# Seven products for eight in a few tile pairs of three down projections, of a float32 transformer stack on one Trainium2 core

## The chip, the cores and the metric

One core of a Trainium2 chip runs the whole program. The metric is device microseconds (us) for one execution; lower is better. Engines: PE is TensorE (PEld its weight loads), DVE is VectorE, ACT is ScalarE, POOL is GpSimd, SP is the queue that issues the weight loads from HBM.

## The reference, cut to what matters

Two transformer blocks on 256 tokens of width 2048, in float32. The change lies in the feed-forward of the first:

```python
hn = rms_norm(h, norm_ffn[i])
h = h + jnp.square(jax.nn.relu(hn @ ffn_w1[i])) @ ffn_w2[i]     # 2048 -> 8192 -> 2048
gate = jax.nn.sigmoid(rms_norm(h, norm_ple[i]) @ ple_w_gate[i])
h = h + (p[i] @ ple_w_proj[i]) * gate
```

## The kernel before

**Precision.** A float32 operand is split in two float32r parts, high and low, and a product is three matmuls: high by high, high by low, low by high. With a stationary of 128x128 (tokens) and a moving operand of 128x512 (weights) that is three matmuls of 512 columns for each tile product.

**The weight pipeline.** All weights come as one stream of 756 pieces of 128x1024 (`PW`). For each piece SP loads it to one of four slots of `raw`; ACT writes the high part to `whi` (`split_hi`, L1833), DVE the low part to `wlo` (`split_lo`, L1115). ACT may write piece q when PE has used piece q-4 (`piece_used`); DVE follows ACT; PE waits for `lo_ready`; SP loads piece q+4 when the low part of piece q is written. Every engine has one queue in program order, and all of them walk through the pieces with `rows_body`: at its step s it first splits piece s+3 and then does what is entered for s.

**The feed-forward** is cut in four chunks of 2048 hidden columns, `chunk(c)`: chunk 0, a loop over chunks 1 and 2, then a small projection (`proj`) and chunk 3. A chunk has 64 pieces. Pieces 0 to 31 are the up stage (`ff`): four groups g of 512 hidden columns, 8 pieces each, in `rows_group` (L550 to L552). Behind each group ACT applies the scale and the relu from two PSUM banks to `z` (`ff_relus`, step 8g+7, L2046), DVE turns it by 32x32 transposes (`ff_turn`, steps 8g+8 and 8g+9, L1515), ACT writes the squares' high part to `H` (`ff_squares`, step 8g+10, L2052), and POOL makes the square once more (L2339) and the low part (L2342), tile by tile, four tiles for each g. Pieces 32 to 63 are the down stage (`fd`): 16 tiles of hidden by 2048 columns, two groups of columns interleaved (`mixed_piece`, L829 to L831), then two more (`rows_group`). DVE adds the sums from PSUM to the residual `xN` (`fd_in`, L1537). A piece is 12 matmuls in both stages.

**PSUM.** The up and down stages use banks 0 to 3 in turn; banks 4 to 7 are free in chunks 0 to 2.

Of the kernel before, what the change touches and what calls it, by code (L numbers as in the profile page):

```python
# [179 lines left out]


def turn_of(n):

    return 4 * (n // 3) + TURN_AT[n % 3]


class Steps:
# [5 lines left out]
    def __call__(self, ins):  # L193
        self.n = self.n + 1
        ins.then_inc(self.sem, 1)
        self.eng.wait_ge(self.sem, self.n)


def program(nc, xT, pT, wstream, consts, setup, params, grows, xrows, out):
# [11 lines left out]
    with ExitStack() as ctx:  # L211
# [45 lines left out]
        zr, sq = ring(bflat, 0), ring(bflat, 4 * S, 8)  # L257
        tA, tB, tC = ring(Sm, 0), ring(Sm, 4 * S), ring(Sm, 8 * S)
        ub, c0 = ring(ptf, 0, 4, S + 4), ring(ptf, 4 * (S + 4), 2)
        sq2 = ring(ptf, 0)  # L260
# [84 lines left out]
        var_most, var_half = sem("var_most"), sem("var_half")  # L345
        ff_turned, ff_hi, ff_step, ff_ready = (sem(n) for n in ("ff_turned", "ff_hi", "ff_step", "ff_ready"))
        fd_sq, fd_turned, fd_hi, a2_ready = (sem(n) for n in ("fd_sq", "fd_turned", "fd_hi", "a2_ready"))
        frs_ready = sem("frs_ready")
# [12 lines left out]
        fin_rs, fin_out, out_done = (sem(n) for n in ("fin_rs", "fin_out", "out_done"))  # L361
        dn_half = sem("dn_half")

        NORM_AT = {"kv": 3, "k2": 0, "up0": 6}
# [96 lines left out]
        def _(pe):  # L461
# [73 lines left out]

            def rows_group(p, p0, u, u0, K, src, ready=None, between={}, upper=False):

                for t in range(QT):
                    if not upper:
# [280 lines left out]
            def mixed_piece(p, p0, u0, src, f, h, ready):  # L820
# [11 lines left out]
                last.then_inc(piece_used, 1)  # L832

            def chunk(c):
                ff, fd, o = chunk_at(c)
                first = {0: lambda: turn_wo(3)} if is_chunk(c, 0) else {}
                for f in range(4):
                    rows_group(o * 64 + (PB[ff] + 8 * f), PB[ff] + 8 * f, o * 16 + (UB[ff] + 2 * f), UB[ff] + 2 * f, DT, A,
                               lambda k: (a1_ready, k + 1), first if f == 0 else {})
                for i, (f, h) in enumerate(WO_FIRST):  # L840
                    if h == 0:
                        pe.wait_ge(z_ready, o * 16 + (UB[fd] + 2 * f + QT))
                    mixed_piece(o * 64 + (PB[fd] + i), PB[fd] + i, UB[fd], H, f, h, lambda k: (ff_ready, c * CH + (k + 1)))
                for f in range(2, 4):
                    late = {}
                    if is_chunk(c, FF_CHUNKS - 1):
                        late = {1: lambda: turn_fd(0), 4: lambda: turn_fd(1)} if f == 2 else {2: lambda: turn_fd(2)}
                    rows_group(o * 64 + (PB[fd] + 8 * f), PB[fd] + 8 * f, o * 16 + (UB[fd] + 2 * f), UB[fd] + 2 * f, CH, H, between=late)
# [10 lines left out]
            for f in range(4):  # L859
                rows_group(PB["proj"] + f, PB["proj"] + f, UB["proj"] + 2 * f, UB["proj"] + 2 * f, 2, pA, upper=(f >= 2))  # L860
            chunk(FF_CHUNKS - 1)
# [247 lines left out]
        def _(dve):  # L1109
            V = nc.vector  # L1110
            dve.sem_inc(z_ready, UB["kv"] + 4)

            def split_lo(i, s):
                dve.wait_ge(hi_ready, i + 1)
                V.tensor_tensor(wlo[:, s, :], raw[:, s, :], whi[:, s, :].bitcast(F32), ALU.subtract).then_inc(lo_ready, 1)  # L1115

# [97 lines left out]

            def rows_body(p, p0, per, groups, evac, between={}, short=0):

                for q in range(LEAD, per * groups + AHEAD):
                    if AHEAD <= q < per * groups + AHEAD - short:
                        split_lo(p + q, (p0 + q) % SLOTS)
                    if q - LEAD in between:  # L1220
# [308 lines left out]
            def chunk(c):  # L1529
# [14 lines left out]
                steps_of.update({32 + WO_FIRST.index((f, 7)): lambda f=f: fd_in(f) for f in range(2)})  # L1544
                steps_of.update({32 + 8 * f + 7: lambda f=f: fd_in(f) for f in range(2, 4)})
                if is_chunk(c, FF_CHUNKS - 1):
                    steps_of.update({51: lambda: fd_lo(0), 54: lambda: fd_lo(1), 60: lambda: fd_lo(2)})
                rows_body(p, PB[ff], 64, 1, lambda f: None, steps_of)

# [10 lines left out]
            def proj_in(f):  # L1560

                if f:
                    dve.wait_ge(z_ready, 4 + UB["proj"] + 2 * f)
                V.tensor_copy(yN[:, 0, f * WIDE:f * WIDE + WIDE], psum[(UB["proj"] + 2 * f) % 4 + f // 2 * 4][:, :]).then_inc(z_ready, 1)
            rows_body(PB["proj"], PB["proj"], 1, 4, proj_in)
# [257 lines left out]
        def _(act):  # L1823
# [5 lines left out]

            def split_hi(i, s, lap):  # L1830
                act.wait_ge(raw_landed[s], lap)
                act.wait_ge(piece_used, i + 1)
                C.copy(whi[:, s, :], raw[:, s, :]).then_inc(hi_ready, 1)  # L1833

            def split(p, p0, i, per, it):

                q = p0 + i
                split_hi(p + i, q % SLOTS, (it * (per // SLOTS) + (q // SLOTS + 1)) * 16)

# [18 lines left out]

            def rows_body(p, p0, it, pieces, between={}, short=0):

                for q in range(LEAD, pieces + AHEAD):
                    if AHEAD <= q < pieces + AHEAD - short:
                        split(p, p0, q, pieces, it)
                    if q - LEAD in between:
# [122 lines left out]
            for i in range(ATT_PIECES + 2):  # L1987
# [31 lines left out]
                if i == 44:  # L2019
                    act.dma_start(tC[:, 0:2, :], pT).then_inc(in_p, 16)  # L2020
                    act.dma_start(gfrow, grows[0].partition_broadcast(P)).then_inc(in_gf, 16)

# [31 lines left out]
            def chunk(c):  # L2054
# [7 lines left out]
                if is_chunk(c, FF_CHUNKS - 1):  # L2062
                    steps_of.update({48: lambda: fd_squares(0), 49: lambda: fd_squares(1), 50: lambda: fd_hi_of(0), 53: lambda: fd_hi_of(1),
                                     56: lambda: fd_squares(2), 59: lambda: fd_hi_of(2)})
                rows_body(PB[ff] + o * 64, PB[ff], o, 64, steps_of)

# [218 lines left out]
        def _(pool):  # L2285
# [226 lines left out]
```

## Time and profile before

| | |
|---|---|
| median of 3 runs | 2207.76 us (2206.84 to 2209.46) |
| the profiled execution's own time | 2206.0 us |
| its span, first to last instruction | 2204.1 us |
| PE busy | 2190.7 us, 99% |
| DVE, ACT, POOL busy | 1518.2, 1092.7, 550.8 us |
| moved by DMA | 414.52 MB, mean 188 GB/s |
| granted TensorE clock | 0.999 |

A busy share says how long an engine had an instruction running. A matmul's duration reaches past the start of the next one, so the rate is read from starts, not from durations. The views named below are the page of the profile, groups of instructions by line, waits by engine, and timelines of one engine.

### The profile page before, as it was taken

How to read it: one execution, taken by the hardware profiler on the slowest of the kernel's cores; microseconds unless marked ns; L12 is line 12 of the kernel's file. 1: busy time of each engine (PE TensorE's matmuls, PEld its weight loads, DVE VectorE, ACT ScalarE, POOL GpSimd, SP SyncE). 2: the span in 40 equal slices, each digit the busy share in tenths (PEclk: the TensorE clock that was granted, in tenths of full speed). 3: DMA queues.
4: the chain of work that ended last, by engine and by line, in shares of the span. 5: the costliest groups of instructions: out<-in, count | busy, mean ns of one | idle time of the engine just before them, and what ended most of it. 6: DMA issues, size and time to landing. Idle time of an engine off the chain costs nothing.

```text
span 2204.1 us, 32431 instructions
## 1 busy us (share of the span) xinstructions
PE 2190.7 (99%) x11111; PEld 1852.5 (84%) x11111; DVE 1518.2 (69%) x2114; ACT 1092.7 (50%) x1622; POOL 550.8 (25%) x467
## 2 busy tenths in 40 slices
PE   9999999999999999999999999999999999999998
PEld 7888988888888788888888887888888888888887
DVE  6877765685586487578566667577774688756875
ACT  6445555544444344444555455465553455434553
POOL 3202220241051043025000033005540244303431
PEclk9999999999999999999999999999999999999999
DMA  7665335556565556556555654545655555555554
GB/s 258 228 228 167 110 130 205 185 178 212 178 204 198 182 181 210 182 183 210 189 182 187 222 167 136 197 155 188 200 190 191 191 190 189 190 194 191 187 208 149
DMA packets 118093, 414.52 MB, mean 188 GB/s; under 512 B 12896, under 2 KB 18048, under 8 KB 117472
## 3 DMA queue, kind: packets, MB, share of 16 engines
q1 hardware_dynamic: 111600, 401.37, 54.0%
q10 hardware_dynamic: 6384, 11.70, 1.7%
q8 instruction: 69, 1.13, 0.2%
q14 instruction: 40, 0.33, 0.0%
HBM read 409.29 MB, written 2.15 MB: 187 GB/s over the span
## 4 chain that ended last, share of the span: by engine, by line
PE 96%; DVE 1%; DMA 1%; POOL 1%; ACT 1%; issue 0%; DVEq 0%; ACTq 0%; SPq 0%; POOLq 0%
PE bank L493 22%; PE bank L501 12%; PE bank L550 10%; PE bank L552 10%; PE bank L551 10%; PE bank L1075 4%; PE bank L1076 4%; PE bank L1074 4%; PE bank L829 3%; PE bank L830 3%; PE bank L831 3%; PE bank L626 1%; PE bank L1009 1%; PE bank L663 1%; PE bank L803 1%; PE bank L805 1%
## 5 line engine op out<-in xcount | busy, mean ns | idle before, releaser
L1115 DVE TENSOR_TENSOR wboth<-raw,wboth 128x1024 fp32r<-128x1024 f32 x756 | 986.0, 1312 | 540.5 <-ACT wboth L1833 538.9
L1833 ACT CAST wboth<-raw 128x1024 fp32r<-128x1024 f32 x756 | 789.4, 1049 | 721.7 <-PE bank L552 231.3
L493 PE MATMUL bank<-A,wboth 128*128 128x512 f32 x1904 | 459.8, 392 | 0.3 <-DVE wboth L1115 0.3
L493 PEld LDWEIGHTS bank<-A,wboth 128*128 128x128 f32 x1904 | 349.2, 188 | 67.8 <-issue 1.0
L501 PEld LDWEIGHTS bank<-A,wboth 128*128 128x128 f32 x1904 | 245.1, 191 | 9.7
L550 PE MATMUL bank<-wboth,A 128*128 128x512 f32 x640 | 250.2, 391 | 2.1 <-issue 1.7
L501 PE MATMUL bank<-A,wboth 128*128 128x256 f32 x1904 | 250.8, 284 | 0.0
L552 PE MATMUL bank<-wboth,A 128*128 128x512 f32 x640 | 249.5, 390 | 0.0
L551 PE MATMUL bank<-wboth,A 128*128 128x512 f32 x640 | 249.3, 390 | 0.0
L2339 POOL TENSOR_TENSOR Sm<-Sm 128x256 f32<-128x256 f32 x64 | 100.9, 1577 | 540.5 <-DVE Sm L1515 540.5
L2296 POOL TENSOR_TENSOR PT<-z,rs 128x256 f32<-128x256 f32 x88 | 73.4, 835 | 465.4 <-DVE z L1146 464.8
L550 PEld LDWEIGHTS bank<-wboth,A 128*128 128x128 f32 x640 | 120.2, 188 | 27.4 <-DVE wboth L1115 1.7
L551 PEld LDWEIGHTS bank<-wboth,A 128*128 128x128 f32 x640 | 120.3, 188 | 25.9 <-issue 1.6
L552 PEld LDWEIGHTS bank<-wboth,A 128*128 128x128 f32 x640 | 120.2, 188 | 25.1
L1076 PE MATMUL bank<-wboth,H 128*128 128x512 f32 x352 | 137.1, 389 | 0.0
L1074 PE MATMUL bank<-wboth,H 128*128 128x512 f32 x352 | 137.1, 389 | 0.0
L1075 PE MATMUL bank<-wboth,H 128*128 128x512 f32 x352 | 137.1, 389 | 0.0
L550 PE MATMUL bank<-wboth,H 128*128 128x512 f32 x320 | 125.2, 391 | 0.0
L552 PE MATMUL bank<-wboth,H 128*128 128x512 f32 x320 | 124.8, 390 | 0.0
L551 PE MATMUL bank<-wboth,H 128*128 128x512 f32 x320 | 124.6, 389 | 0.0
L1515 DVE STREAM_TRANSPOSE Sm<-z 32x256 f32<-32x256 f32 x256 | 111.5, 436 | 4.2
L829 PE MATMUL bank<-wboth,H 128*128 128x512 f32 x256 | 99.9, 390 | 0.0
(299 smaller groups left out, 2990.9 us busy)
## 6 DMA issues: line engine op xcount, KB each, us to landing
raw<-wstream SPq DMA_DIRECT2D x756, 512.0 KB, 3.3
bias<-bias_rows ACTq DMA_DIRECT2D x6, 512.0 KB, 5.3
x<-xrows ACTq DMA_DIRECT2D x1, 2048.0 KB, 9.1
bias<-grows ACTq DMA_DIRECT2D x2, 1024.0 KB, 5.7
out<-x SPq DMA_DIRECT2D x8, 256.0 KB, 2.1
x<-xT SPq DMA_DIRECT2D x7, 256.0 KB, 5.2
pA<-bias_rows ACTq DMA_DIRECT2D x2, 512.0 KB, 10.1
Sm<-grows ACTq DMA_DIRECT2D x1, 1024.0 KB, 6.1
```

Of the source, the lines that this page charges most:

```text
L493: last = nc.tensor.matmul(bank(j)[:, :], whi[:, s, cols(i)], moving(j, k), start=(k == 0), stop=(k == K - 1))
L501: last = nc.tensor.matmul(bank(j)[:, 0:S], wlo[:, s, cols(i)], moving(j, k)[:, 0, :], start=False, stop=False)
L550: nc.tensor.matmul(bank[:, :], src[:, k, 0, tok], whi[:, s, w], start=(k == 0), stop=False)
L551: nc.tensor.matmul(bank[:, :], src[:, k, 0, tok], wlo[:, s, w], start=False, stop=False)
L552: last = nc.tensor.matmul(bank[:, :], src[:, k, 1, tok], whi[:, s, w], start=False, stop=(k == K - 1))
L829: nc.tensor.matmul(bank[:, :], src[:, k, 0, tok], whi[:, p0 % SLOTS, w], start=(k == 0), stop=False)
L1074: nc.tensor.matmul(bank[:, :], H[:, k, 0, tok], whi[:, s, w], start=(k == 0), stop=False)
L1075: nc.tensor.matmul(bank[:, :], H[:, k, 0, tok], wlo[:, s, w], start=False, stop=False)
L1076: return nc.tensor.matmul(bank[:, :], H[:, k, 1, tok], whi[:, s, w], start=False, stop=(k == n - 1))
L1115: V.tensor_tensor(wlo[:, s, :], raw[:, s, :], whi[:, s, :].bitcast(F32), ALU.subtract).then_inc(lo_ready, 1)
L1515: last = V.transpose(cols[:, :, :, 32 * i:32 * i + 32], rows[:, :, :, 32 * j:32 * j + 32])
L1833: C.copy(whi[:, s, :], raw[:, s, :]).then_inc(hi_ready, 1)
```

## The change

Chunks 0 to 2 take another down stage, `down_pair`. The weights come by pairs of column groups: a piece is one hidden tile by 1024 columns, 16 pieces for each of two column pairs (`cp`). For two of the eight pairs of hidden tiles (`FAST`: pairs 3 and 5) the eight tile products (two token tiles, two hidden tiles, two column groups) become seven products of sums of blocks. In each chunk four groups of pieces are of that kind; they begin at pieces 38, 42, 54 and 58 (`X_AT`). The sums:

- of hidden tiles (`mix`): three small sums on POOL behind its four tiles of g = 1 and g = 2, a high part of 128x512 on ACT (`mix_high`, steps 22 and 30), a low part on POOL.
- of weights (`t_first`, `t_rest`): two sums of 128x512 on DVE at step x-4, two on POOL; the high parts on ACT in two halves at step x-2 (`t_highs`), the low parts on DVE before it splits piece x+2 (`t_lows`). Before DVE splits piece x+1 it waits for POOL's two.
- of results: the seventh products stand in four extra PSUM banks, `side_bank`. DVE adds them at steps 44 and 60 (`sides_in`), POOL makes three more adds (`corners`), DVE adds the main banks (`mains_in`). Main and side banks swap between the two column pairs, so all eight are used.

Of pieces 38, 42, 54 and 58 only the first half is split. The projection swaps its two halves of PSUM, and the load of a 1 MB row of gains (`gfrow`) moves from the attention to just ahead of the projection. Chunk 3 stays as it was.

```diff
+FAST = ((3, 5), (3, 5))
+MIXED = sorted({m for ms in FAST for m in ms})
+GROUPS = [(cp, n, m) for cp, ms in enumerate(FAST) for n, m in enumerate(ms)]
+X_AT = {32 + 16 * cp + 2 * m: g for g, (cp, n, m) in enumerate(GROUPS)}
...
+                def group(i, g):
+
+                    _, n, m = GROUPS[g]
+                    lone, final = n == 0, n == len(FAST[cp]) - 1
...
+                    product(side_bank(cp, ONE), *hidden(i, early), *weights(i, 0), lone, final).then_inc(piece_used, 1)
+                    arrive(i + 1)
+                    product(main_bank(cp, 0), *hidden(i + 1, early), *weights(i + 1, 0))
+                    pe.wait_ge(*mix_ready.at(c * len(MIXED) + (MIXED.index(m) + 1)))
+                    product(main_bank(cp, 2), *mix_of(m, 3), *weights(i + 1, 1)).then_inc(piece_used, 1)
+                    pe.wait_ge(*t_lo.at(2 * group_of(c, g) + 1))
+                    product(side_bank(cp, FIVE), *mix_of(m, 1), *sums(0), lone, final)
+                    product(side_bank(cp, SEVEN), *mix_of(m, 0), *sums(1), lone, final)
+                    pe.wait_ge(*t_lo.at(2 * group_of(c, g) + 2))
+                    product(side_bank(cp, SIX), *mix_of(m, 2), *sums(2), lone, final)
+                    product(main_bank(cp, 1), *hidden(i + 1, late), *sums(3)).then_inc(t_used.sem, 1)
...
+                if cp:
+                    for i in (14, 15):
+                        arrive(i)
+                        last = plain(i, 0)
+                    last.then_inc(first_half.sem, 1)
+                    for i in (14, 15):
+                        plain(i, 1).then_inc(piece_used, 1)
```

DVE:

```diff
+                steps_of.update({x - 4: lambda x=x, g=g: t_first(c, x, g) for x, g in X_AT.items()})
+                ahead = {x + 1: lambda g=g: dve.wait_ge(*t_more.at(2 * group_of(c, g) + 2)) for x, g in X_AT.items()}
+                ahead.update({x + 2: lambda g=g: t_lows(c, g) for x, g in X_AT.items()})
+                steps_of.update({44: lambda: sides_in(c, 0), 49: lambda: mains_in(c, 0, range(4)), 60: lambda: sides_in(c, 1),
+                                 62: lambda: mains_in(c, 1, range(2)), 63: lambda: mains_in(c, 1, range(2, 4))})
+                rows_body(p, PB[ff], 64, 1, lambda f: None, steps_of, 0, ahead, X_AT)
```

ACT:

```diff
+                steps_of.update({8 * (m // 2) + 14: lambda n=n, m=m: mix_high(c, n, m) for n, m in enumerate(MIXED)})
+                steps_of.update({x - 2: lambda g=g: t_highs(c, g) for x, g in X_AT.items()})
+                steps_of.update({44: lambda: copy_side(c, 0), 60: lambda: copy_side(c, 1)})
...
+            def mix_high(c, n, m):
+
+                act.wait_ge(*mix_sum.at(c * 3 * len(MIXED) + (3 * n + 3)))
+                if not is_chunk(c, 0):
+                    act.wait_ge(*t_used.at(group_of(c, 0)))
+                C.copy(mixed[0][:, m // 2, :, :], mixsum[:, m // 2, :, :]).then_inc(mix_hi.sem, 1)
+
+            def t_highs(c, g):
+
+                act.wait_ge(*t_sum.at(2 * group_of(c, g) + 2))
+                if g or not is_chunk(c, 0):
+                    act.wait_ge(*t_used.at(group_of(c, g)))
+                C.copy(Tcopy[0][:, 0:2, :], Tsum[:, 0:2, :]).then_inc(t_hi.sem, 1)
+                act.wait_ge(*t_more.at(2 * group_of(c, g) + 2))
+                C.copy(Tcopy[0][:, 2:4, :], Tsum[:, 2:4, :]).then_inc(t_hi.sem, 1)
```

POOL, in `chunk(c)`:

```diff
                         G.tensor_tensor(part(H, 4 * g + j, 1), tB[:, j, :], part(H, 4 * g + j, 0).bitcast(F32),
                                         ALU.subtract).then_inc(ff_ready, 1)
+                    if 2 * g + 1 in MIXED and not is_last(c):
+                        mix(c, MIXED.index(2 * g + 1), g)
+                if not is_last(c):
+                    for cp in range(2):
+                        for x, g in X_AT.items():
+                            if GROUPS[g][0] == cp and x > 34:
+                                t_rest(c, x, g)
+                        corners(c, cp)
...
+            def mix(c, n, g):
...
+                G.tensor_tensor(dst[:, 0:2, :], ends_of, a[:, late].unsqueeze(1).to_broadcast([P, 2, P]), ALU.subtract).then_inc(mix_sum.sem, 1)
+                pool.wait_ge(*mix_sum.at(s0 + 1))
+                G.tensor_tensor(dst[:, 2, :], dst[:, 1, :], a[:, early], ALU.add).then_inc(mix_sum.sem, 1)
+                pool.wait_ge(*mix_sum.at(s0 + 2))
+                G.tensor_tensor(dst[:, 3, :], b[:, early], dst[:, 2, :], ALU.subtract).then_inc(mix_sum.sem, 1)
+                pool.wait_ge(*mix_sum.at(s0 + 3))
+                pool.wait_ge(*mix_hi.at(c * len(MIXED) + (n + 1)))
+                G.tensor_tensor(mixed[1][:, g, :, :], dst, mixed[0][:, g, :, :].bitcast(F32), ALU.subtract).then_inc(mix_ready.sem, 1)
```

## Rows read from the trace of the kernel before

**Rows 1.** The page: busy time of engines, granted clock in 40 slices.

```profile
PE 2190.7 (99%) x11111; PEld 1852.5 (84%) x11111; DVE 1518.2 (69%) x2114; ACT 1092.7 (50%) x1622; POOL 550.8 (25%) x467
...
PEclk9999999999999999999999999999999999999999
```

**Rows 2.** PE's waits from 390 to 1100 us: total, times, longest.

```profile
PE bank L550 <- issue: 1.7, 2, 1.4
```

**Rows 3.** PE's timeline: start us, duration us, engine, instruction.

```profile
473.05 0.40 PE L550 MATMUL bank<-wboth,A 128*128 128x512 f32 x1
...
481.23 0.39 PE L829 MATMUL bank<-wboth,H 128*128 128x512 f32 x1
...
481.91 0.39 PE L829 MATMUL bank<-wboth,H 128*128 128x512 f32 x1
```

**Rows 4.** ACT's timeline in chunk 0, groups g = 1 and 2.

```profile
450.98 2.93 ACT L1833 CAST wboth<-raw 128x1024 fp32r<-128x1024 f32 x3
454.43 1.05 ACT L1833 CAST wboth<-raw 128x1024 fp32r<-128x1024 f32 x1 [0.51 <-DMA raw<-wstream]
456.98 1.05 ACT L1833 CAST wboth<-raw 128x1024 fp32r<-128x1024 f32 x1 [1.51 <-PE bank L552]
459.65 1.27 ACT L2046 ACTIVATE z<-bank,nrm 128x512 f32<-128x512 f32 x2 [1.62 <-PE bank L552]
460.80 1.05 ACT L1833 CAST wboth<-raw 128x1024 fp32r<-128x1024 f32 x1
```

**Rows 5.** POOL's timeline: end of g = 1, then g = 2 and 3.

```profile
458.68 1.59 POOL L2339 TENSOR_TENSOR Sm<-Sm 128x256 f32<-128x256 f32 x1
460.35 0.73 POOL L2342 TENSOR_TENSOR H<-Sm,H 128x256 fp32r<-128x256 f32 x1
...
482.15 0.74 POOL L2342 TENSOR_TENSOR H<-Sm,H 128x256 fp32r<-128x256 f32 x1
493.37 1.65 POOL L2339 TENSOR_TENSOR Sm<-Sm 128x256 f32<-128x256 f32 x1 [10.48 <-DVE Sm L1515]
...
503.94 0.74 POOL L2342 TENSOR_TENSOR H<-Sm,H 128x256 fp32r<-128x256 f32 x1
```

**Rows 6.** POOL's timeline in chunk 1, a square with DVE idle.

```profile
654.85 0.61 POOL L2339 TENSOR_TENSOR Sm<-Sm 128x256 f32<-128x256 f32 x1
```

**Rows 7.** DVE's timeline in chunk 0, g = 2 and 3.

```profile
452.05 7.75 DVE L1115 TENSOR_TENSOR wboth<-raw,wboth 128x1024 fp32r<-128x1024 f32 x5 [1.09 <-ACT wboth L1833]
461.88 1.23 DVE L1115 TENSOR_TENSOR wboth<-raw,wboth 128x1024 fp32r<-128x1024 f32 x1 [2.08 <-ACT wboth L1833]
463.02 3.59 DVE L1515 STREAM_TRANSPOSE Sm<-z 32x256 f32<-32x256 f32 x8
...
471.54 1.22 DVE L1115 TENSOR_TENSOR wboth<-raw,wboth 128x1024 fp32r<-128x1024 f32 x1
...
489.68 3.61 DVE L1515 STREAM_TRANSPOSE Sm<-z 32x256 f32<-32x256 f32 x8
```

**Rows 8.** DVE's timeline in chunk 0, splits of pieces 37 to 42.

```profile
493.32 1.23 DVE L1115 TENSOR_TENSOR wboth<-raw,wboth 128x1024 fp32r<-128x1024 f32 x1
495.64 7.75 DVE L1115 TENSOR_TENSOR wboth<-raw,wboth 128x1024 fp32r<-128x1024 f32 x5 [1.09 <-ACT wboth L1833]
```

**Rows 9.** Groups by line and shape: busy us, mean ns, idle before.

```profile
L1537 DVE TENSOR_TENSOR x<-x,bank 128x512 f32<-128x512 f32 x32 | 20.6, 684 | 6.1 <-PE bank L831 3.1 <-PE bank L552 3.1
...
L2326 POOL TENSOR_TENSOR Sm<-Sm,small 128x512 f32<-128x512 f32 x16 | 20.0, 1267 | 24.2 <-DVE small L1292 24.1
...
L1580 DVE TENSOR_TENSOR y<-x,Sm 128x512 f32<-128x512 f32 x8 | 5.5, 691 | 0.3
...
L1949 ACT CAST wboth<-raw 128x512 fp32r<-128x512 f32 x1 | 0.6, 604 | 0.0
```

More of the change, by code:

```diff
@@ L534, in spread_rs, with rows_group @@
                 nc.tensor.matmul(psum[4][:, 0:S], ones[:, :], acc[:, :], start=True, stop=True).then_inc(sum_ready, 1)
-            def rows_group(p, p0, u, u0, K, src, ready=None, between={}, upper=False):
+            def rows_group(p, p0, u, u0, K, src, ready=None, between={}, upper=False, free=False):
                 for t in range(QT):
-                    if not upper:
+                    if not free:
                         pe.wait_ge(z_ready, u + t + 1)
@@ L832, in mixed_piece, with product, down_pair, weights @@
                 last.then_inc(piece_used, 1)
+            def product(bank, a_hi, a_lo, w_hi, w_lo, start=False, stop=False):
+                nc.tensor.matmul(bank[:, :], a_hi, w_hi, start=start, stop=False)
+                nc.tensor.matmul(bank[:, :], a_hi, w_lo, start=False, stop=False)
+                return nc.tensor.matmul(bank[:, :], a_lo, w_hi, start=False, stop=stop)
+            def down_pair(c, cp):
+                _, fd, o = chunk_at(c)
+                p, z0 = o * 64 + (PB[fd] + 16 * cp), o * 16 + (4 + UB[fd])
+                early, late = slice(0, P), slice(P, 2 * P)
+                def weights(i, f):
+                    s, w = (PB[fd] + 16 * cp + i) % SLOTS, slice(f * WIDE, f * WIDE + WIDE)
+                    return whi[:, s, w], wlo[:, s, w]
+                def hidden(i, tok):
+                    return H[:, i, 0, tok], H[:, i, 1, tok]
+                def mix_of(m, i):
+                    return mixed[0][:, m // 2, i, :], mixed[1][:, m // 2, i, :]
+                def sums(i):
+                    return Tcopy[0][:, i, :], Tcopy[1][:, i, :]
+                def arrive(i):
+                    pe.wait_ge(lo_ready, p + (i + 1))
+                    if cp == 0:
+                        pe.wait_ge(ff_ready, c * CH + (i + 1))
+                def plain(i, f):
+                    for t in range(QT):
+                        last = product(main_bank(cp, 2 * f + t), *hidden(i, slice(t * P, t * P + P)), *weights(i, f), i == 0, i == 15)
+                    return last
+                def group(i, g):
+                    _, n, m = GROUPS[g]
+                    lone, final = n == 0, n == len(FAST[cp]) - 1
+                    if lone and cp == 0:
+                        pe.wait_ge(z_ready, z0)
+                    if lone and cp:
+                        pe.wait_ge(*banks_taken.at(c * 8 + 4))
+                    product(side_bank(cp, ONE), *hidden(i, early), *weights(i, 0), lone, final).then_inc(piece_used, 1)
[10 more added lines that the diff above has]
+                if cp:
+                    pe.wait_ge(z_ready, z0 + 4)
+                elif not is_chunk(c, 0):
+                    pe.wait_ge(*banks_taken.at(c * 8))
+                for i in range(16 - 2 * cp):
+                    g = X_AT.get(32 + 16 * cp + i)
+                    if X_AT.get(32 + 16 * cp + i - 1) is not None:
+                        continue
+                    arrive(i)
+                    if g is not None:
+                        group(i, g)
+                    else:
+                        plain(i, 0)
+                        plain(i, 1).then_inc(piece_used, 1)
+                if cp:
+                    for i in (14, 15):
+                        arrive(i)
+                        last = plain(i, 0)
+                    last.then_inc(first_half.sem, 1)
+                    for i in (14, 15):
+                        plain(i, 1).then_inc(piece_used, 1)
@@ L1213, in take_rs, with rows_body @@
                     dve.wait_ge(rs_ready, then)
[L1215 removed]
+            def rows_body(p, p0, per, groups, evac, between={}, short=0, ahead={}, halves=()):
                 for q in range(LEAD, per * groups + AHEAD):
+                    if q in ahead:
+                        ahead[q]()
                     if AHEAD <= q < per * groups + AHEAD - short:
[L1219 removed]
+                        split_lo(p + q, (p0 + q) % SLOTS, WIDE if q in halves else PW)
                     if q - LEAD in between:
@@ new lines, in t_lows, with sides_in @@
+            def t_lows(c, g):
+                for h in range(2):
+                    two = slice(2 * h, 2 * h + 2)
+                    dve.wait_ge(*t_hi.at(2 * group_of(c, g) + (h + 1)))
+                    V.tensor_tensor(Tcopy[1][:, two, :], Tsum[:, two, :], Tcopy[0][:, two, :].bitcast(F32), ALU.subtract).then_inc(t_lo.sem, 1)
+            def sides_in(c, cp):
+                _, fd, o = chunk_at(c)
+                done = banks_taken.sem if cp else z_ready
+                dve.wait_ge(*t_used.at(group_of(c, len(FAST[0]) + (len(FAST[1]) if cp else 0))))
+                if cp or not is_chunk(c, 0):
+                    dve.wait_ge(*corners_added.at(c * 6 + 3 * cp))
+                one, five, six, seven = (side_bank(cp, j)[:, :] for j in range(4))
+                V.tensor_tensor(quarter(cp, 1, 0), quarter(cp, 1, 0), seven, ALU.add).then_inc(done, 1)
+                V.tensor_tensor(quarter(cp, 1, 1), quarter(cp, 1, 1), seven, ALU.subtract).then_inc(done, 1)
+                dve.wait_ge(*side_copied.at(c * 2 + (cp + 1)))
+                V.tensor_tensor(quarter(cp, 0, 0), quarter(cp, 0, 0), one, ALU.add).then_inc(done, 1)
+                V.tensor_tensor(corner, six, cross, ALU.subtract).then_inc(side_step.sem, 1)
+                dve.wait_ge(*side_step.at(c * 2 + (cp + 1)))
+                V.tensor_tensor(cross, corner, five, ALU.subtract).then_inc(done, 1)
@@ L1857, in body, with rows_body @@
                                     step(j)
-            def rows_body(p, p0, it, pieces, between={}, short=0):
+            def rows_body(p, p0, it, pieces, between={}, short=0, halves=()):
                 for q in range(LEAD, pieces + AHEAD):
                     if AHEAD <= q < pieces + AHEAD - short:
-                        split(p, p0, q, pieces, it)
+                        split(p, p0, q, pieces, it, WIDE if q in halves else PW)
                     if q - LEAD in between:
@@ L2335, in chunk @@
                 for g in range(4):
+                    if g == 3 and 34 in X_AT and not is_last(c):
+                        t_rest(c, 34, X_AT[34])
                     pool.wait_ge(ff_turned, c * 16 + (4 * g + 4))
```

132 lines of the change are left out of this document (112 added, 20 removed).

## The prediction

> **What bounds the kernel.** I read the page first. PE is busy for 2190.7 of 2204.1 us and the granted clock stands at 9 in all forty slices, which is the 2.4 GHz level [rows 1]. Then PE's waits in the four chunks: 1.7 us at the turn of the loop, and nothing above 0.3 us besides [rows 2]. So fewer matmuls are worth their full time, as long as no other engine falls behind.
>
> The timelines tell how near that is. The start of one triple and of the next in the down stage are 481.23 and 481.91: 0.227 us for a matmul, 2.72 us for a piece of twelve. The down stage of chunk 0 begins at 481.23, so piece 29 begins at 481.23 - 3 x 2.72 = 473.07, and a row shows it at 473.05 [rows 3]. DVE ends the low part of piece 29 at 471.54 + 1.22 = 472.76 [rows 7]: 0.3 us ahead. In the same way piece 37 begins at 481.23 + 5 x 2.72 = 494.83 and its low part is done at 493.32 + 1.23 = 494.55 [rows 8]: 0.3 us again. The reader is to see that after each group's relu and transposes DVE has no lead left, though it is busy for only 69% of the span [rows 1]. The chain is: relu (ACT), low part of the next piece and eight transposes, a low part, eight transposes, a low part (DVE). Whatever delays the relu by more than 0.3 us delays PE.
>
> **What it removes.** Each group of two pieces has 21 matmuls in place of 24. Four groups in three chunks: 12 x 3 x 0.227 = 8.2 us off PE. Shapes and strides of the matmuls are those of before, so I give each the 0.227 us.
>
> **First wait: the sums of hidden tiles, at g = 1 and g = 2.** ACT is to make the high part at step 22, that is behind the split of piece 25 at 454.43 and ahead of the split of piece 26 (456.98) and of the relu of g = 2 (459.65) [rows 4]. It waits there for three sums that POOL makes only behind its four tiles of g = 1, and these end at 460.35 + 0.73 = 461.08 [rows 5]. Queued behind the waiting ACT are the split of piece 26, the relu, and piece 27.
>
> Step by step: DVE lacks piece 26's high part and idles from 452.05 + 4 x 1.55 = 458.25 [rows 7], so POOL's last square takes 0.61 us [rows 6] instead of 1.59 and its last low part ends at 460.1. Of the sums one has 256 columns, 0.74 us as L2342, and two have 128. For these no row stands; from 0.74 at 256 and 1.27 at 512 [rows 9] I estimate 0.47 each. With some 0.08 us between instructions the sums end at 462.0. High part 0.60 [rows 9], piece 26 1.05, relu 1.27 with piece 27 beginning 1.15 after it, piece 27 1.05 [rows 4]: DVE can start piece 27 at 465.95, where it started at 461.88 [rows 7]. That is 4.1 us late, of which 0.3 are covered: 3.8 us of PE. Piece 26 itself costs nothing more, since its low part (464.9) comes when PE reaches it (464.9).
>
> At g = 2 the same happens: POOL ends its tiles at 482.15 + 0.74 = 482.9 [rows 5], 21.8 us behind g = 1 as all else, and the high part is at step 30. DVE and POOL have both moved by the first delay, and nothing is covered now: 4.1 us. Bounds for each of the two: 3.2 us if the small sums cost next to nothing, 5.5 us if POOL shares its time with DVE, since a square takes 1.59 us beside DVE's splits and 0.61 alone [rows 5, 6].
>
> The Trainium skill (GPSIMD Engine Reference, Specifications) says that POOL's way into SBUF is shared with VectorE and contended by DVE instructions that have two SBUF inputs. The splits are such, and the trace agrees (1.59 against 0.61 us). By that rule a waiting DVE makes POOL quick, which gives the lower of my two prices, about 4 us; if POOL had the same speed whatever DVE does, each wait would be 5.5 us and the whole some 9 us longer.
>
> **Second wait: the sums of weights at piece 38.** DVE may not split piece 39 before POOL has made its two sums, and these stand in POOL's queue behind all four tiles of g = 3. Call T the end of the last transposes (489.68 + 3.61 = 493.29 before [rows 7]). POOL began those tiles at 493.37 and ended them at 503.94 + 0.74 = 504.68, or T + 11.4 [rows 5]; PE reaches the second matmul triple of piece 38 at 494.83 + 2.72 + 0.68 = 498.23, T + 4.9.
>
> With the change: DVE's low part of 37 ends at T + 1.3, the two sums (0.69 each, as L1580 [rows 9]) at 2.65, half of piece 38 at 3.35, and then it waits. POOL's first tile and the start of the second run beside DVE: 1.65 + 1.6 us. The rest runs alone: 0.61 + 0.74 with 0.05 between, 1.4 us a tile, so the fourth ends at T + 7.6. The two sums have 512 columns, 1.27 us each [rows 9] and one waits for the other: T + 10.4. Low part of 39: T + 11.65. PE started piece 37 at T + 1.3, piece 38 at 4.0, and stands after three matmuls at 4.7: **7.0 us of wait**. The 18 other matmuls end at T + 15.8; DVE has by then made both low parts of the sums (12.9, 14.1) and piece 40 (15.3), so nothing is added. ACT, which waits for the same POOL, gives the high parts at 11.5 and 12.6. Bounds: 5 us (POOL's sums at half price), 9 us (its tiles at the pace beside DVE for longer).
>
> **The other three groups.** For piece 42 the same queue has POOL free: DVE's sums, half a split, POOL's 2.8 us, then piece 43. I count 0.4 us of wait, since DVE had just caught up. For 54 and 58 DVE has its full lead of about three pieces (8 us), of which two sums, POOL and two low parts of 1.23 us take about 6: no wait; with POOL slowed, up to 1 us.
>
> **Results.** Five adds of 0.68 us (L1537 [rows 9]) at step 44 and at step 60 are 3.4 us, beside four plain pieces of PE (10.9 us). At the end of a chunk the first two main banks must be free for the next up stage: PE gives them 12 matmuls (2.72 us) ahead, DVE needs 2 x 0.68 and about 0.4 of signal: 1 us to spare. If that cover were gone it would cost its excess, three times. `corners` is POOL's, DVE waits for it at step 49 with about two pieces of lead. The 1 MB row of gains is some 5 us of DMA between pieces that land 5 us ahead of need: nothing. The projection's swap of banks waits for adds that are past by then: nothing. The order of weights changes no byte. Half splits of 12 pieces save ACT and DVE time that is off the path.
>
> **Sum.** Per chunk 3.8 + 4.1 + 7.0 + 0.4 = 15.3 us; three chunks 45.9; less 8.2: **+37.7 us**. Against the profiled execution: 2206.0 + 37.7 = 2243.7 us, and the median stands 1.8 above it: 2245.5 us.
>
> **Rivals.**
>
> - *Only the wait at piece 38 bites.* If ACT's wait for the small sums were covered (POOL being done earlier than its rows say), 3 x 7.4 - 8.2 = +14: 2222 us. Against it: POOL's end at 461.08 is 1.4 us behind the relu that it now holds, and DVE has 0.3 us. Chance 0.10.
> - *The clock falls in the waits.* Before, PE never stands over 1.7 us in these chunks and the granted clock never leaves 2.4 GHz, so no row shows what 7 us of rest do. At the 1.2 GHz level a matmul costs 0.227 us more; if the 18 behind each long wait ran so, 3 x 18 x 0.227 = +12 us: 2258 us. Part of that would hide behind DVE's own work in the same stretch (3.6 us of the 4.1). The Trainium skill (TensorE: Matmul & The Clock Gate, Part 1) says that a TensorE without work is throttled to half rate until it has been busy again for a while; by it this rival would hold, and its price is the one above. Chance 0.12.
> - *None of the waits bites: faster.* 2207.8 - 8.2 = 2199.6 us. One thing decides it: POOL, whose spans are rough. It is so if POOL has finished g = 3 and its two sums by T + 3.4, 7 us ahead of my reckoning; between, the change breaks even where a chunk waits 2.7 us in all. Four tiles at the fastest rows, 1.4 us each, already take 5.6 us. Chance 0.06.
> - *No change*, the waits near 2.7 us a chunk: 0.02.
>
> **Numbers.** The forecast has 0.70. With bounds: 3 x (3.2 + 3.2 + 5.0 + 0) - 8.2 = +26, 2234 us, and 3 x (5.5 + 5.5 + 9 + 2) - 8.2 = +58, 2266 us. The range takes in the first rival below and the clock's above: 2221 to 2262 us. What this kernel's measurement can tell from no change is about 0.2%, 4.4 us. Faster 0.06, within 0.2% 0.02, slower 0.92.
>
> **What would show it.** In the profile after: PE's waits should list, three times each, about 7 us at the triple behind piece 38's first (releaser DVE's split L1115), and two smaller groups of waits, 4 us in all each, at pieces 28 and 29 and at 36 and 37. ACT's high part of the hidden sums should wait for POOL, and relu rows should come about 4 us later against the up stage's end of g. POOL's squares of g = 3 should shrink from 1.59 to 0.61 us. PE should have 36 matmuls fewer and its pitch of 0.227 us kept. The prediction is wrong if PE does not wait at piece 39 although POOL's second weight sum ends late, or if POOL's rows of the trace are not where its work ended.

## The result and the profile after

| | before | after |
|---|---|---|
| median | 2208.05 us (4 runs) | 2246.86 us (4 runs, 2246.29 to 2247.87) |
| profiled execution, own time / span | 2206.0 / 2204.1 us | 2247.87 / 2246.0 us |
| mean granted clock | 0.999 | 0.991 |

The changed kernel takes 1.018 times as long, 95% interval [1.0168, 1.0192]; the medians are 38.8 us apart. Forecast were 2245.5 us. The profiled execution is the longest of the four, 1.0 us above their median.

The page of the changed kernel first, against [rows 1]:

```profile
PE 2199.5 (98%) x11075; PEld 1851.4 (82%) x11075; DVE 1572.6 (70%) x2192; ACT 1115.0 (50%) x1658; POOL 620.7 (28%) x533
...
PEclk9999999999999998999999999999999999999999
```

PE has 36 matmuls fewer and is busy for 8.8 us longer: the busy time of a matmul grows when its clock is low, and the clock's row has an 8 now. PE's waits from 385 to 1110 us, against [rows 2] (total, times, longest):

```profile
PE bank L893 <- DVE wboth L1260: 24.2, 10, 6.2
PE bank L607 <- DVE wboth L1260: 9.0, 9, 1.9
PE bank L607 <- ACT y L2316: 0.8, 1, 0.8
PE bank L607 <- issue: 0.6, 1, 0.6
```

L893 is the down stage, L607 the up stage, L1260 the split of the weights that was L1115: 33 us of waiting where there was next to none. More than that was lost, 41.9 + 8.2 = 50.1 us: a listed wait is counted from the modelled end of the matmul before it (0.39 us behind its start, where the next one would start after 0.227), the first start behind a wait comes some 0.1 us slower, and time at a low clock is no wait. The starts of the stages in PE's timeline place it all:

| us from first matmul to the next stage's | before | after | more |
|---|---|---|---|
| up stages of chunks 0, 1, 2 | 88.0, 87.2, 89.0 | 91.9, 91.0, 92.9 | 3.9, 3.8, 3.9 |
| down stages of chunks 0, 1, 2 | 87.0, 87.6, 87.2 | 97.3, 97.8, 96.4 | 10.2, 10.2, 9.3 |
| projection | 11.4 | 11.9 | 0.5 |

The sum is 41.7 of the 41.9 us between the two spans. The start of piece 37 divides the down stages: up to it, where the delay of g = 2 ends, PE is later by 3.6, 3.7 and 2.1 us, and from there to the end by 6.6, 6.5 and 7.2 us although 2.7 us of matmuls are gone, so that 9.4, 9.2 and 9.9 us are lost there. Chunk 2 has other parts: the 3.9 us of its up stage are 3.7 up to piece 29 and 1.8 of low clock behind it, less 1.6 us (1.4 as the list counts) that PE had waited at the loop's turn before [rows 2] and now does not; coming late by the clock, PE waits less in the down stage.

The projection's 0.5 us is one of ACT's copies that PE waits for (0.8 us here, 0.3 before); ahead of it a split by DVE beside POOL's `corners` of chunk 2 took 1.71 us and not 1.23. No run tried what made the copy late.

**The wait on ACT, chunk 0, g = 1 to 2.** ACT's timeline, which stands against [rows 4], then POOL's against [rows 5], then DVE's against [rows 7]:

```profile
454.79 1.06 ACT L2038 CAST wboth<-raw 128x1024 fp32r<-128x1024 f32 x1 [0.53 <-DMA raw<-wstream]
462.24 0.62 ACT L2288 CAST vT<-kT 128x512 fp32r<-128x512 f32 x1 [6.40 <-POOL kT L2599]
462.77 1.04 ACT L2038 CAST wboth<-raw 128x1024 fp32r<-128x1024 f32 x1
463.72 1.26 ACT L2250 ACTIVATE z<-bank,nrm 128x512 f32<-128x512 f32 x2
```

```profile
459.00 0.61 POOL L2575 TENSOR_TENSOR Sm<-Sm 128x256 f32<-128x256 f32 x1
459.70 0.74 POOL L2578 TENSOR_TENSOR H<-Sm,H 128x256 fp32r<-128x256 f32 x1
460.39 0.74 POOL L2595 TENSOR_TENSOR kT<-Sm 128x256 f32<-128x256 f32 x1
461.21 0.46 POOL L2597 TENSOR_TENSOR kT<-kT,Sm 128x128 f32<-128x128 f32 x1
461.75 0.46 POOL L2599 TENSOR_TENSOR kT<-Sm,kT 128x128 f32<-128x128 f32 x1
```

```profile
465.94 1.23 DVE L1260 TENSOR_TENSOR wboth<-raw,wboth 128x1024 fp32r<-128x1024 f32 x1 [0.63 <-ACT wboth L2038]
467.09 3.60 DVE L1662 STREAM_TRANSPOSE Sm<-z 32x256 f32<-32x256 f32 x8
...
475.61 1.22 DVE L1260 TENSOR_TENSOR wboth<-raw,wboth 128x1024 fp32r<-128x1024 f32 x1
```

The reader is to see three engines handing on one delay: ACT idles for 6.40 us until POOL's third small sum, its relu comes at 463.72 instead of 459.65, DVE splits piece 27 at 465.94 instead of 461.88 and piece 29 at 475.61 instead of 471.54. Each is 4.1 us late.

**The wait on POOL, chunk 0, piece 38.** Here T, the end of the last transposes, is 497.50 + 3.61 = 501.11. POOL's timeline, DVE's, PE's:

```profile
501.19 1.65 POOL L2575 TENSOR_TENSOR Sm<-Sm 128x256 f32<-128x256 f32 x1 [11.42 <-DVE Sm L1662]
...
508.17 0.72 POOL L2578 TENSOR_TENSOR H<-Sm,H 128x256 fp32r<-128x256 f32 x1
508.85 1.26 POOL L2608 TENSOR_TENSOR PT<-PT,raw 128x512 f32<-128x512 f32 x1
510.19 1.26 POOL L2610 TENSOR_TENSOR PT<-PT,raw 128x512 f32<-128x512 f32 x1
```

```profile
497.50 3.61 DVE L1662 STREAM_TRANSPOSE Sm<-z 32x256 f32<-32x256 f32 x8
...
503.31 1.23 DVE L1714 TENSOR_TENSOR PT<-raw 128x512 f32<-128x512 f32 x1
...
511.48 1.23 DVE L1260 TENSOR_TENSOR wboth<-raw,wboth 128x1024 fp32r<-128x1024 f32 x1 [5.92 <-POOL PT L2610]
```

```profile
502.42 0.50 PE L893 MATMUL bank<-wboth,H 128*128 128x512 f32 x1 [1.88 <-DVE wboth L1260]
...
504.77 0.63 PE L895 MATMUL bank<-wboth,H 128*128 128x512 f32 x1
505.20 0.63 PE L893 MATMUL bank<-wboth,H 128*128 128x512 f32 x1
...
512.76 0.79 PE L893 MATMUL bank<-wboth,H 128*128 128x512 f32 x1 [5.03 <-DVE wboth L1260]
...
514.21 0.63 PE L893 MATMUL bank<-wboth,vT 128*128 128x512 f32 x1
514.63 0.63 PE L894 MATMUL bank<-wboth,vT 128*128 128x512 f32 x1
...
519.24 0.39 PE L893 MATMUL bank<-wboth,H 128*128 128x512 f32 x1
```

POOL's second sum ends at 511.45, T + 10.3; DVE idles 5.92 us for it and splits piece 39 at T + 10.4. PE's starts are 0.43 us apart at 504.77, and again at 514.21: the clock is at its lower level. Piece 40 begins at 519.24, T + 18.1. The windows of the same stretch (us, then busy time of each engine, granted clock, DMA share, GB/s):

```profile
504.00:508.00 4.00, 3.73 (x10) 2.55 (x8) 1.56 (x2) 1.04 (x1) 3.84 (x5) 0.58 0.61 200
508.00:512.00 4.00, 0.00 (x0) 0.00 (x0) 0.52 (x1) 0.52 (x1) 3.29 (x4) 0.85 0.10 39
512.00:516.00 4.00, 3.24 (x8) 2.56 (x9) 4.00 (x4) 2.94 (x4) 0.00 (x0) 0.50 0.41 131
```

Granted are 0.58 and 0.50 of 2.4 GHz, so 1.2 GHz for most of the first and all of the last. It fell first behind waits of 0.88 and 1.88 us, the second of which ended 4.9 us after the first, and was low again behind the 5.03. Of the 18 matmuls behind the long wait 11 start at the low pace in chunk 0, 9 in chunk 1 and 14 in chunk 2; the clock is back before the group ends.

### The profile page after: what moved, and what is told of

Its sections match the earlier page's. It is cut to its first block, busy times and chain, and to the rows that moved or that the text cites. A ratio compares the mean times of both kernels' runs of the same rounds, so it can differ in the third digit from the quotient of the medians.

```text
span 2246.0 us, 32721 instructions
## 1 busy us (share of the span) xinstructions
PE 2199.5 (98%) x11075; PEld 1851.4 (82%) x11075; DVE 1572.6 (70%) x2192; ACT 1115.0 (50%) x1658; POOL 620.7 (28%) x533
## 4 chain that ended last, share of the span: by engine, by line
PE 71%; issue 20%; POOL 6%; DVE 1%; ACT 1%; DMA 0%; POOLq 0%; DVEq 0%; ACTq 0%
PE bank L550 22%; PE bank L558 12%; PE bank L1220 4%; PE bank L1221 4%; PE bank L1219 4%; PE bank L607 3%; PE bank L609 3%; PE bank L608 3%; POOL Sm L2575 2%; POOL H L2578 1%; PE bank L893 1%; PE bank L894 1%; PE bank L895 1%; PE bank L663 1%; PE bank L664 1%
## 5 line engine op out<-in xcount | busy, mean ns | idle before, releaser
L1260 DVE TENSOR_TENSOR wboth<-raw,wboth 128x1024 fp32r<-128x1024 f32 x756 | 979.0, 1303 | 530.5 <-ACT wboth L2038 487.2
L607 PE MATMUL bank<-wboth,A 128*128 128x512 f32 x640 | 251.6, 393 | 10.4 <-DVE wboth L1260 9.0
L2530 POOL TENSOR_TENSOR PT<-z,rs 128x256 f32<-128x256 f32 x88 | 73.5, 836 | 465.5 <-DVE z L1291 464.9
L2575 POOL TENSOR_TENSOR Sm<-Sm 128x256 f32<-128x256 f32 x64 | 88.5, 1382 | 328.3 <-DVE Sm L1662 328.3
L607 PEld LDWEIGHTS bank<-wboth,A 128*128 128x128 f32 x640 | 120.5, 188 | 40.5 <-DVE wboth L1260 9.2
L893 PE MATMUL bank<-wboth,H 128*128 128x512 f32 x312 | 124.8, 400 | 24.3 <-DVE wboth L1260 24.2
L1220 PE MATMUL bank<-wboth,H 128*128 128x512 f32 x352 | 136.9, 389 | 0.0
L1219 PE MATMUL bank<-wboth,H 128*128 128x512 f32 x352 | 136.9, 389 | 0.0
L1221 PE MATMUL bank<-wboth,H 128*128 128x512 f32 x352 | 136.9, 389 | 0.0
L894 PE MATMUL bank<-wboth,H 128*128 128x512 f32 x312 | 123.6, 396 | 0.0
L895 PE MATMUL bank<-wboth,H 128*128 128x512 f32 x312 | 123.3, 395 | 0.0
L1291 DVE TENSOR_REDUCE z<-bank 128x256 f32<-128x512 f32 x108 | 74.2, 689 | 27.5 <-PE bank L550 27.3
```

The costliest lines, as they stand in the source:

```text
L893: nc.tensor.matmul(bank[:, :], a_hi, w_hi, start=start, stop=False)
L894: nc.tensor.matmul(bank[:, :], a_hi, w_lo, start=False, stop=False)
L1219: nc.tensor.matmul(bank[:, :], H[:, k, 0, tok], whi[:, s, w], start=(k == 0), stop=False)
L1220: nc.tensor.matmul(bank[:, :], H[:, k, 0, tok], wlo[:, s, w], start=False, stop=False)
L1221: return nc.tensor.matmul(bank[:, :], H[:, k, 1, tok], whi[:, s, w], start=False, stop=(k == n - 1))
L1260: V.tensor_tensor(wlo[:, s, 0:w], raw[:, s, 0:w], whi[:, s, 0:w].bitcast(F32), ALU.subtract).then_inc(lo_ready, 1)
```

## The experiments

Every time is a median. Every ratio is against the kernel before as it ran beside the experiment, with its 95% interval. That kernel's own median was 2208.05 us beside the change, 2205.94 beside e1 to e4, 2207.94 beside e5 to e7 and 2206.51 beside e8 and e9. So a difference between two kernels of different groups is uncertain by some 2 us; where it matters, the difference of the excesses over the kernel before stands with it.

**e1: ACT makes the high part of the hidden sums three steps later.**

```diff
-                steps_of.update({8 * (m // 2) + 14: lambda n=n, m=m: mix_high(c, n, m) for n, m in enumerate(MIXED)})
+                steps_of.update({8 * (m // 2) + 17: lambda n=n, m=m: mix_high(c, n, m) for n, m in enumerate(MIXED)})
```

> One edit: ACT makes the high part of the hidden sums three steps later (25 and 33), behind the relu and the split of piece 28 or 36. Theory (ACT, waiting for POOL, holds the relu, and DVE has no lead): the waits at pieces 28/29 and 36/37, 3.7 us each in the trace of the change, go, 3 x 7.4 = 22 us, and the low clock behind the wait at piece 37 with them; the wait at piece 39 stays near 5 to 7 us. 2221 to 2226 us. Rival (the sums' load on POOL and ACT is what costs, wherever it stands): the time stays within 3 us of 2247.

Measured: 2224.17 us, ratio 1.0084 [1.0068, 1.0099]. ACT's timeline:

```profile
459.37 1.27 ACT L2250 ACTIVATE z<-bank,nrm 128x512 f32<-128x512 f32 x2 [1.61 <-PE bank L609]
...
463.73 0.62 ACT L2288 CAST vT<-kT 128x512 fp32r<-128x512 f32 x1 [0.53 <-POOL kT L2599]
```

The same sums now cost ACT 0.53 us of idling, and the up stages are about as long as before (88.1, 87.5, 87.7 us against 88.0, 87.2, 89.0, of which the last held 1.6 us more at the loop's turn). 22.7 us are back, as expected (20.6 by the excesses, 18.2 us in place of 38.8), and the rival falls: it is the order, not the work. The wait at piece 39 is longer in the record, 6.2 us, since the products ahead of it now run at full clock.

**e2: POOL makes the weight sums of pieces 38 and 42 earlier**, between its tiles.

```diff
-                    if g == 3 and 34 in X_AT and not is_last(c):
-                        t_rest(c, 34, X_AT[34])
+                    if g == 3 and 38 in X_AT and not is_last(c):
+                        t_rest(c, 38, X_AT[38])
...
                     for j in range(4):
+                        if g == 3 and j == 2 and not is_last(c):
+                            t_rest(c, 42, X_AT[42])
...
-                            if GROUPS[g][0] == cp and x > 34:
+                            if GROUPS[g][0] == cp and x > 42:
```

> One edit, on POOL alone: its two weight sums for piece 38 stand ahead of the four tiles of g = 3, and those for piece 42 between the second tile and the third. Theory (DVE waits at piece 39 for POOL's queue): the sums end at T + 5.7 instead of T + 11.4 or 10.4, T being the end of the last transposes; the wait at piece 39 falls from 5.0 us at its recorded length to about 2.3, the 15 to 20 matmuls at half clock around it are mostly gone; waits at 28/29 and 36/37 stay. 2223 to 2231 us. Rival (POOL's sums are slow wherever they stand, because DVE shares its way): the wait moves to pieces 42 to 45 and the time stays above 2238.

Measured: 2234.81 us, ratio 1.0132 [1.0117, 1.0148]. A miss by half: 12 us back (9.9 by the excesses) instead of 16 to 24, above my window and below the rival's. DVE's timeline shows why:

```profile
506.09 1.62 DVE L1260 TENSOR_TENSOR wboth<-raw,wboth 128x1024 fp32r<-128x1024 f32 x1 [2.54 <-POOL PT L2612]
507.63 3.31 DVE L1721 TENSOR_TENSOR Tboth<-PT,Tboth 128x1024 fp32r<-128x1024 f32 x2
510.86 2.89 DVE L1260 TENSOR_TENSOR wboth<-raw,wboth 128x1024 fp32r<-128x1024 f32 x2
```

The wait for POOL is 2.54 us. But POOL's tiles now run beside DVE's group work: a split takes 1.62 us and the two low parts 3.31, where in the changed kernel they took 1.23 and 2.35. A second wait of 0.7 us follows at piece 43 in chunks 0 and 1. PE's wait at piece 39 was to be 2.3 us; it is so in chunk 2 alone (2.28). In chunks 0 and 1 it is 0.66, because the clock still fell ahead of it, behind the waits at pieces 36 and 37, and PE came late.

**e3: both edits.**

> Both edits. If the two waits are separate mechanisms in series the gains add: 2208 - 8.2 + 3 x 2.3 = 2207 us, between 2203 and 2211; if they are one, the time is that of the better of the two, 2221 or more.

Measured: 2213.81 us, ratio 1.0033 [1.0021, 1.0045]. The gains add, 22.7 and 12.1 against 33.1 us for both (20.6 and 9.9 against 30.9 by the excesses), so the two waits are separate; the time is 7 us above the forecast and 3 us outside its window. Its up stages are as before; its down stages are longer by 2.4, 2.8 and 2.8 us where I had 2.3 - 2.7 = -0.4. Waits of 2.2 to 2.3 us at piece 39 and 0.7 at 43 in two chunks explain 0.7 of that; the rest are late starts of up to 0.3 us each inside the groups, some 1.9 us a down stage, and in chunk 2 six matmuls at the lower clock.

**e4: both edits, and no group at piece 38**; **e9** is the same kernel once more, beside e8.

```diff
-FAST = ((3, 5), (3, 5))
+FAST = ((5,), (3, 5))
```

> Both edits, and the pair at piece 38 is left to the plain eight products: three groups a chunk instead of four, 27 matmuls fewer than before instead of 36. Theory: 2208 - 6.1 and no wait left over 0.5 us: 2202 to 2204 us, faster than both kernels. Rival (a group costs more at its own place than the 0.68 us it saves): no faster than the kernel before.

> The three groups with both orders mended once more, on the same chip as the one above, to compare the two: 2201 us, 0.2% below the kernel before; the other is faster only if its fourth group costs less than 0.68 us a chunk.

Measured: 2201.21 us, ratio 0.9977 [0.9968, 0.9986]; again 2201.33 us, ratio 0.9973 [0.9963, 0.9983]. PE's waits from 385 to 1010 us hold no split any more:

```profile
PE bank L607 <- ACT y L2316: 0.8, 1, 0.8
PE bank L607 <- issue: 0.6, 1, 0.6
```

This version is faster than both kernels, than the one before by 0.2%. The seven products give most of what they save once no split is waited for: 27 matmuls are 6.1 us, 4.7 and 5.2 us are measured. Half a microsecond of the rest is PE's wait for ACT's copy in the projection, which stands here too.

**e5: PE works through the long wait.**

```diff
                     product(side_bank(cp, ONE), *hidden(i, early), *weights(i, 0), lone, final).then_inc(piece_used, 1)
+                    if g == 0:
+                        for _ in range(22):
+                            nc.tensor.matmul(side_bank(cp, SIX)[:, :], A[:, 0, 0, 0:P], A[:, 0, :, :], start=True, stop=True)
                     arrive(i + 1)
```

> The changed kernel, and behind the first three matmuls of piece 38 PE runs 22 matmuls on operands at hand into the bank of the sixth product, whose own first product starts that bank anew later; they fill 5.0 us of the wait and compute nothing that is used. Theory (the engine's rest lets the granted clock fall to 1.2 GHz, and the products behind run at half the pace): the clock stays at 2.4 GHz through piece 38, the end of group 38 comes at T + 15.8 instead of T + 18.1, and the time falls by 3 x 2.3 = 7 us, to 2240 us (2237 to 2243). Rival (the low clock hides behind DVE's own steps, as the prediction had it for most): 2245 to 2249 us.

Measured: 2239.56 us, ratio 1.0148 [1.0132, 1.0163], 7.3 us less than the changed kernel (7.2 by the excesses) with 66 matmuls more. Here T is 500.46. The windows of the wait and of the products behind it, and PE's first matmul of piece 40:

```profile
508.00:512.00 4.00, 2.92 (x13) 2.07 (x12) 1.07 (x1) 1.07 (x2) 2.81 (x3) 1.00 0.00 0
512.00:516.00 4.00, 3.79 (x17) 3.13 (x18) 4.00 (x5) 2.94 (x4) 0.00 (x0) 1.00 0.34 133
```

```profile
516.44 0.39 PE L893 MATMUL bank<-wboth,H 128*128 128x512 f32 x1
```

The clock stays at 1.00, and DVE splits piece 39 at 510.93, T + 10.5, where the changed kernel has T + 10.4. DVE's wait is the same, only the clock of PE behind it differs. Piece 40 begins at T + 16.0, 16.1 and 16.1 us in the three chunks, in the changed kernel at T + 18.1, 18.0 and 18.9: 2.1, 1.8 and 2.8 us, 6.7 of the 7.3. The low clock does not hide.

**e6: the list of pairs alone.** The edit of e4 without the two orders.

> Only the list of pairs: the pair at piece 38 takes the plain eight products, orders on ACT and POOL stay as in the change. Theory: the waits at 28/29 and 36/37 stay (7.4 us a chunk), the wait at 39 is gone, and the group at 42, whose POOL sums stand behind the tiles of g = 3, waits little (under 1 us): 2206 + 3 x (7.4 + 1.2 of low clock - 2.0) + 1 = 2227 us, 2222 to 2231. Rival (piece 38 is no special place; the wait moves to piece 43): 2240 us or more.

Measured: 2224.57 us, ratio 1.0073 [1.0057, 1.0088]. The waits at pieces 28, 29, 36 and 37 stand (8.7 us in the up stages, 7.6 in the down stages, all but 0.6 us at these four), and there is none at 39 nor at 43, though POOL's sums for 42 still stand behind its tiles. The clock falls here without any long wait, once in each chunk. A window of chunk 0, behind the waits of 0.87 and 1.88 us at pieces 36 and 37; then, in chunk 1, the wait at piece 37 with none at 36 ahead of it, and the window behind it:

```profile
504.00:508.00 4.00, 3.88 (x10) 3.10 (x11) 2.92 (x4) 3.00 (x4) 3.84 (x4) 0.57 0.50 147
```

```profile
685.56 0.49 PE L893 MATMUL bank<-wboth,H 128*128 128x512 f32 x1 [1.89 <-DVE wboth L1260]
```

```profile
688.00:692.00 4.00, 4.00 (x19) 3.33 (x18) 4.00 (x3) 2.01 (x3) 3.84 (x4) 1.00 0.71 201
```

**e7: four groups, the fourth at piece 50; both orders mended.**

```diff
-FAST = ((3, 5), (3, 5))
+FAST = ((5,), (1, 3, 5))
...
-                steps_of.update({44: lambda: sides_in(c, 0), 49: lambda: mains_in(c, 0, range(4)), 60: lambda: sides_in(c, 1),
+                steps_of.update({44: lambda: sides_in(c, 0), 48: lambda: mains_in(c, 0, range(4)), 60: lambda: sides_in(c, 1),
```

> Four groups a chunk again, with the fourth at piece 50 (pair 1 in the second column pair) instead of 38, both orders mended, and the main banks of the first column pair taken in a step earlier (48). Theory (a group costs nothing where DVE has its lead and POOL is free): 36 matmuls fewer, 2206 - 8.2 + 1 to 2 of loose ends = 2199 us, 2197 to 2201. Rival (with three groups in sixteen pieces DVE's lead is used up, or PE waits at piece 50 for the main banks): 2203 us or more.

Measured: 2216.65 us, ratio 1.0041 [1.0027, 1.0055]: a miss. PE waits 3.4 to 3.5 us at piece 50 in every chunk, for the adds of the main banks, L1753. DVE's timeline:

```profile
528.38 0.68 DVE L1260 TENSOR_TENSOR wboth<-raw,wboth 128x512 fp32r<-128x512 f32 x1
531.62 1.23 DVE L1260 TENSOR_TENSOR wboth<-raw,wboth 128x1024 fp32r<-128x1024 f32 x1 [2.56 <-POOL PT L2612]
532.76 2.47 DVE L1753 TENSOR_TENSOR x<-x,bank 128x512 f32<-128x512 f32 x4
```

The rival had named this wait; its cause I had not counted: DVE waits for POOL's weight sums of piece 50 at its step for piece 51, and the adds stand right behind.

**e8: the same with the main banks taken one step earlier,** ahead of that wait (47 instead of 48).

> As the kernel with a group at piece 50, but DVE takes the main banks of the first column pair at step 47 instead of 48, that is before it waits for POOL's weight sums of piece 50. Theory (the 3.4 us wait at piece 50 is the order in DVE's queue: mains behind the wait for POOL): the wait falls to 0 to 1 us a chunk, the low clock behind it goes, 2216.7 - 3 x (3 to 3.5) - 3 to 6 of clock: 2200 to 2204 us. Rival (POOL's corner adds end too late for any order): 2212 us or more.

Measured: 2202.01 us, ratio 0.9980 [0.9971, 0.9989]:

```profile
526.75 0.68 DVE L1260 TENSOR_TENSOR wboth<-raw,wboth 128x512 fp32r<-128x512 f32 x1
527.36 2.47 DVE L1753 TENSOR_TENSOR x<-x,bank 128x512 f32<-128x512 f32 x4
530.01 1.23 DVE L1260 TENSOR_TENSOR wboth<-raw,wboth 128x1024 fp32r<-128x1024 f32 x1 [0.18 <-POOL PT L2612]
```

The adds fill the time in which DVE waited for POOL (0.18 us instead of 2.56 are left). 14.6 us come back from one step's place (13.2 by the excesses). Of waits for splits 1.0 us is left in three places. Beside e9 (2201.33 us) there is no difference that the measurement can tell: the fourth group's 2.0 us are spent. Its three down stages together are 0.4 us longer than e9's, where 2.0 less was due; 1.0 of that is those waits, and the rest stays without a place.

## Why the prediction was right, point by point

- **That nothing else bounds the kernel, and 8.2 us off PE.** Right: 36 matmuls fewer, the same 0.227 us between starts at full clock; e4 bears it out, with 4.7 and 5.2 of 6.1 us.
- **The first wait, 3.8 us at g = 1.** Measured 3.9, 3.8, 3.9 us in the three up stages, the last of other parts, as said above. The steps of the sum held to 0.4 us: POOL's sums end at 462.2 (forecast 462.0), the low part of piece 26 at 465.3 (464.9, so that it did cost PE 0.3 us), piece 27's split starts at 465.94 (465.95); 128 columns take 0.46 us (0.47). The cause is shown by e1.
- **The same at g = 2, 4.1 us.** Measured 3.6 and 3.7 us in chunks 0 and 1, and 2.1 in chunk 2, where PE came late by the clock. The last transposes end at 501.11 and not 493.29: DVE is 7.8 us late in all, 4.1 since g = 1 and 3.8 more since g = 2. The 4.1 hold 0.3 us by which this execution ran later already (POOL begins the tiles of g = 1 at 450.12, before at 449.78), so each wait held DVE for 3.8 us where the sum had 4.1. The waits (0.88 and 1.88 us in chunk 0) are like those at g = 1 (0.92 and 1.92).
- **The second wait.** DVE splits piece 39 at T + 10.4, as forecast. One step under it was wrong without effect: DVE's two sums, beside POOL's tiles, took 1.10 and 1.23 us and not 0.69 each, which its wait for POOL swallowed. The recorded waits are 5.0, 5.2 and 6.2 us and not 7.0; in chunks 0 and 1 the matmuls ahead ran at half pace and came late themselves. At full clock it is 6.2 us in e1 too: PE stands from T + 5.3 there and not from 4.7. Cause shown by e2 and by e6.
- **The group's end, T + 15.8.** The step that failed: it is T + 18.1, 18.0 and 18.9. The forecast let the products behind the wait run at full clock and gave the low clock to a rival of chance 0.12, saying that part of it would hide. The clock did fall in each chunk, which is that rival's mechanism. The rival charged 4.1 us a group, 18 matmuls at the low pace; 11, 9 and 14 ran so, which is 1.8 to 2.8 us, and e5 shows that none of it hid. So the forecast's term, nothing for the clock, was 7 us short and the rival's 12 us were 5 too many. With the clock kept up (e5) the group ends at T + 16.0 to 16.1: the rest of that sum was right.
- **0.4 us at piece 42, 0 to 1 us at 54 and 58.** No wait there; 1.2 us of the forecast were not spent.
- **Results and projection at nothing.** Right but for 0.5 us in the projection.
- **The sum.** 37.7 us forecast, 41.9 between the spans, 38.8 between the medians. The clock's 7 us stand against smaller losses at g = 2 (2.9 us in all), no wait at 42 (1.2) and a shorter wait at the loop's turn. That the median came out within 1.4 us is in part luck: errors of opposite sign, and a median that rose by 3 us less than the span of the profiled executions did. The stated range, up to 2262 us, also left out the sum of the upper bounds, 2266.
- **POOL beside a waiting DVE.** Of POOL's four squares of g = 3 the first took 1.65 us and the second 1.06 beside DVE's work, the last two 0.61 with DVE waiting; I had 1.65 and 1.6 for the first and the start of the second. The Trainium skill (GPSIMD Engine Reference, Specifications) has the SBUF interfaces shared between the two and contended by DVE instructions with two SBUF inputs: the trace agrees.
- **The clock behind a rest.** Behind the long wait the granted clock was 0.50. The Trainium skill (TensorE: Matmul & The Clock Gate, Part 1) has a TensorE without work throttled: the trace agrees, and e5 shows the price here.

What stays open is when the short waits bring the clock down. That they can is shown by e6: with the waits at pieces 28 and 29 and at 36 and 37 and no long one, the clock fell once a chunk, each time behind such a pair. In e1, without them, it fell once a chunk behind the long wait alone, and in e4 it stayed up. But in the changed kernel and in e6 alike only three of five such pairs were followed by a fall; the one in the up stage of chunk 0 was not, in either. Two lone waits of 1.9 us (piece 37 in chunk 2 of the changed kernel, in chunk 1 of e6) were followed by none; in the changed kernel the next one came only in the long wait. What decides between them no run shows.

## What to carry to other kernels

An engine at 69% can have no lead at all at one place. Find that place by comparing when an operand is ready with when it is used; a wait put into any queue ahead of it costs what it exceeds the lead by, and the same work at another step next to nothing (22.7 us for three steps later in e1, 14.6 us for one earlier in e8). Before a product is saved on the bound engine, follow every sum that it needs through the queue in which it is made, and leave out the places where that queue is busy: three groups at good places beat four with one at a bad one by 12.6 us (e4 against e3).

## What the runs showed of the hardware

- The granted clock fell to 1.2 GHz although PE's waits before it were only 0.88 and 1.88 us (e6, where no longer one exists: 0.57 over 504 to 508 us); starts of matmuls were then 0.43 us apart. Keeping PE at work that nobody needs through a wait of 5 to 6 us was worth 1.8 to 2.8 us each time (e5).
- POOL and DVE slow each other in both directions. POOL: a square of 128x256 in 0.61 us alone and 1.59 beside splits. DVE: a sum of 128x512 from SBUF in 0.68 us alone (e2), 1.10 and 1.23 beside POOL's tiles (the changed kernel, at the same step), 1.78 beside its 512-column adds (e7); a split of 128x1024 in 1.23 us alone and up to 2.14 beside those adds (the changed kernel, 721.54).
